# The first compression matmul with its operands exchanged: window tokens stationary in four column groups

## What is computed

```python
CMP_LEN, CMP_STRIDE, CMP_HIDDEN = 32, 16, 256        # S = 256 tokens, HEAD_DIM 64, G = 2 groups
n_cmp = (S - CMP_LEN) // CMP_STRIDE + 1              # 15 windows
cmp_idx = cmp_start[:, None] + np.arange(CMP_LEN)[None, :]

def compress(t, pe, w1, w2):
    blk = t[:, cmp_idx] + pe[:, None, :]
    blk = jnp.moveaxis(blk, 3, 2).reshape(B, n_cmp, G, CMP_LEN * D)
    return jax.nn.gelu(blk @ w1) @ w2

kc = rope_partial(compress(k_cmp, cmp_pos_k, cmp_wk1, cmp_wk2), pos[:, cmp_end])
vc = compress(v_cmp, cmp_pos_v, cmp_wv1, cmp_wv2)
```

## Time and profile before

| | us |
|---|---|
| median of 3 runs | 2285.81 |
| the three runs | 2283.96, 2285.81, 2295.26 |
| span of the profiled execution | 2275.8 |
| PE busy | 1985.1 (87%) |
| DVE busy | 871.2 (38%) |
| ACT busy | 735.0 (32%) |

### The profile page before, as it was taken

How to read it: one execution, slowest core, us unless ns; L and a number is a source line. 1 busy time by engine, 2 the same in 40 slices (tenths; PEclk the granted TensorE clock), 3 DMA queues, 4 the chain that set the end, 5 groups by cost and what they waited for, 6 DMA issues and landing times.

```text
span 2275.8 us, 29449 instructions
## 1 busy us (share of the span) xinstructions
PE 1985.1 (87%) x11980; PEld 1551.8 (68%) x11980; DVE 871.2 (38%) x1464; ACT 735.0 (32%) x1018; POOL 119.3 (5%) x112
## 2 busy tenths in 40 slices
PE   7967798888898777999988879987799998797997
PEld 5844443334443377778887879877787888797986
DVE  3052121111221232533355756533343335575653
ACT  1230011111111132557345434322255634533432
POOL 0000000000000000320210000000031030000000
PEclk9987899999999975999999989998599999998999
DMA  5403588988988732223223334543123322342452
GB/s 208 178 1 157 233 352 337 379 368 360 375 361 359 321 139 107 75 98 126 78 109 148 130 114 180 202 168 141 75 75 111 112 111 101 123 148 112 186 192 102
DMA packets 30887, 412.36 MB, mean 181 GB/s; under 512 B 3600, under 2 KB 5040, under 8 KB 5808
## 3 DMA queue, kind: packets, MB, share of 16 engines
q1 hardware_dynamic: 30768, 410.68, 46.0%
HBM read 408.84 MB, written 1.84 MB: 180 GB/s over the span
## 4 chain that ended last, share of the span: by engine, by line
issue 86%; PE 6%; POOL 5%; DVE 1%; DMA 1%; ACT 0%; SPq 0%; POOLq 0%; DVEq 0%; ACTq 0%
POOL work_mem L1650 5%; PE bank L703 3%; PE bank L711 2%; DMA work_mem<-in_const 1%; PE bank L798 0%; PE bank L735 0%; PE bank L780 0%; POOL small L1658 0%; PE bank L737 0%; PE bank L738 0%; DVE ht_mem L1689 0%; PE bank L773 0%; DVE work_mem L1809 0%; POOL small L1631 0%; DVE work_mem L1826 0%
## 5 line engine op out<-in xcount | busy, mean ns | idle before, releaser
L926 PE MATMUL bank<-wring,gates_mem 128*64 128x512 f32 x1024 | 238.5, 623 | 47.3 <-DMA wring<-in_w 40.7
L2012 DVE TENSOR_TENSOR w_lo<-wring,w_hi 128x2048 fp32r<-128x2048 f32 x88 | 201.3, 2292 | 188.2 <-ACT w_hi L1445 188.2
L1445 ACT ACTIVATE w_hi<-wring 128x2048 fp32r<-128x2048 f32 x88 | 168.5, 1915 | 303.4 <-PE bank L1002 171.8
L1001 PE MATMUL bank<-mixed_hi,w_hi_early 128*128 128x256 f32 x960 | 243.7, 291 | 6.8 <-DVE mixed_lo L2020 4.2
L1445 ACT ACTIVATE w_hi_early<-wring 128x2048 fp32r<-128x2048 f32 x80 | 152.9, 1912 | 265.3 <-PE bank L1002 176.1
L1002 PE MATMUL bank<-mixed_lo,w_hi_early 128*128 128x256 f32 x960 | 238.3, 285 | 0.0
L2012 DVE TENSOR_TENSOR w_lo<-wring,w_hi_early 128x2048 fp32r<-128x2048 f32 x80 | 183.2, 2290 | 124.7 <-ACT w_hi_early L1445 124.7
L926 PEld LDWEIGHTS bank<-wring,gates_mem 128*64 128x64 f32 x1024 | 88.4, 143 | 192.3 <-issue 192.3
L1006 PE MATMUL bank<-mixed_hi,w_lo 128*128 128x256 f32 x1472 | 208.8, 285 | 0.0
L1001 PEld LDWEIGHTS bank<-mixed_hi,w_hi_early 128*128 128x128 f32 x960 | 186.3, 194 | 12.3 <-issue 6.1
L1006 PEld LDWEIGHTS bank<-mixed_hi,w_lo 128*128 128x128 f32 x1472 | 192.2, 194 | 0.0
(11 more groups left out here) (404 smaller groups left out, 3216.2 us busy)
## 6 DMA issues: line engine op xcount, KB each, us to landing
wring<-in_w SPq DMA_DIRECT2D x192, 2048.0 KB, 8.4
cst<-in_const SPq DMA_DIRECT2D x1, 1273.0 KB, 7.6
prm<-in_prm SPq DMA_DIRECT2D x3, 381.0 KB, 8.5
x_mem<-in_x SPq DMA_DIRECT2D x1, 1024.0 KB, 4.9
out_x<-x_mem SPq DMA_DIRECT2D x1, 1024.0 KB, 3.9
rel_skew<-work_mem SPq DMA_DIRECT2D x1, 768.0 KB, 3.5
work_mem<-in_prm SPq DMA_DIRECT2D x1, 512.0 KB, 12.3
work_mem<-rel_skew SPq DMA_DIRECT2D x1, 512.0 KB, 3.6
```

What stands on the lines that cost most here:

```text
L926: mm = pe.matmul(out[half, :], x_e[:, pair, k, half], w[e][:, k, :], start=(k == 0), stop=(k == KT - 1))
L1001: pe.matmul(out, w[0][:, k, cols], x[0][:, k, :], start=(k == 0), stop=False)
L1445: act.activation(hi, w, ACT.Copy).then_inc(hi_ready, 1)
L2012: dve.tensor_tensor(lo, w, hi, ALU.subtract).then_inc(lo_ready, 1)
```

## The change

In each `hid` job the operands are exchanged. The stationary operand is now the windows' tokens: 31 columns, the 15 windows of either group and one meaningless window between them; the moving operand is a row block of the weights, 256 columns. The 16 steps of the contraction go in turn to four column groups q of the array, whose results lie in PSUM partitions 32q to 32q+30 of the same bank; each group adds up four steps. The four partial sums have to be added and turned, since they are windows x hidden and the rest of the kernel wants hidden x windows. ACT copies each of them, 31x256, into its 32 partitions of a new tile `hid_parts` (in `gates_mem`), and two new jobs `hsum` multiply a 128-column half of it, stationary, by a constant 0/1 matrix `winsum` (128x30) as the moving operand, which has a one where partition mod 32 is the window's row. The result is the 128x60 bank that was there before, and ACT copies it as before. DVE sets `hid_parts` to zero at the start of each layer, since partition 31 of each group is never written. The table of constants grows by the 30 columns of `winsum` and is loaded by the same DMA.

```diff
     ("negtriu", 256), ("gla", 7 * 128), ("rope", 128), ("dup", 256), ("inv", 1), ("cmpmask", 2 * N_CMP),
-    ("rowvalid", 2), ("iota", CAP), ("neghalf", 8), ("ones8", 8), ("one", 1), ("bucket", 384))
+    ("rowvalid", 2), ("iota", CAP), ("neghalf", 8), ("ones8", 8), ("one", 1), ("winsum", 2 * N_CMP), ("bucket", 384))
...
+    c[:, CONST["winsum"]] = row % 32 == (np.arange(2 * N_CMP) + np.arange(2 * N_CMP) // N_CMP)[None]
...
-                        ("rope_k", 1), ("dup", 2), ("hid", 2), ("kc", 1), ("vc", 1), ("rope_c", 1), ("gla_la", 1),
+                        ("rope_k", 1), ("dup", 2), ("hid", 2), ("hsum", 2), ("kc", 1), ("vc", 1), ("rope_c", 1), ("gla_la", 1),
...
-    pc_T = view(gates_mem, 6144, HEADS, S)
+    pc_T, hid_parts = view(gates_mem, 6144, HEADS, S), view(gates_mem, 0, 2, CMP_HIDDEN)
...
                 pe.wait_ge(dup_ready, 8 * l + 4 * n + 4)
                 free(j, l)
+                for step in range(4):
+                    for q in range(4):
+                        k = 4 * step + q
+                        win = dup[:, 2 * n + k // 8, :].rearrange("p (c s) -> p c s", s=CMP_STRIDE)
+                        mm = pe.matmul(psum[j.bank][32 * q:32 * q + 2 * N_CMP + 1, 0:CMP_HIDDEN],
+                                       win[:, k // 8:k // 8 + 2 * N_CMP + 1, 2 * (k % 8)], w[:, k, :],
+                                       start=(step == 0), stop=(step == 3))
+                mm.then_inc(bank_full[j.bank], 1)
+            for n, j in enumerate(layer["hsum"]):
+                parts_read = layer["hid"][n]
+                pe.wait_ge(bank_read[parts_read.bank], parts_read.count(l))
+                free(j, l)
                 for half in range(2):
-                    for k in range(16):
-                        win = dup[:, 2 * n + k // 8, :].rearrange("p (g c s) -> p g c s", g=2, s=CMP_STRIDE)
-                        mm = pe.matmul(psum[j.bank][:, half * 30:half * 30 + 30].rearrange("p (g c) -> p g c", g=2),
-                                       w[:, k, half * P:(half + 1) * P],
-                                       win[:, :, k // 8:k // 8 + N_CMP, 2 * (k % 8)], start=(k == 0), stop=(k == 15))
+                    mm = pe.matmul(psum[j.bank][:, half * 2 * N_CMP:(half + 1) * 2 * N_CMP],
+                                   hid_parts[:, n, half * P:(half + 1) * P], C("winsum"), start=True, stop=True)
                 mm.then_inc(bank_full[j.bank], 1)
...
+            act.wait_ge(hid_parts_clear, l + 1)
             for n, j in enumerate(layer["hid"]):
+                full(j, l)
+                for q in range(4):
+                    rows = slice(32 * q, 32 * q + 2 * N_CMP + 1)
+                    ins = act.activation(hid_parts[rows, n, :], psum[j.bank][rows, 0:CMP_HIDDEN], ACT.Copy)
+                ins.then_inc(bank_read[j.bank], 1)
+            for n, j in enumerate(layer["hsum"]):
                 full(j, l)
                 act.activation(hid_c[:, n].rearrange("p a b -> p (a b)"), psum[j.bank][:, 0:4 * N_CMP], ACT.Copy).then_inc(bank_read[j.bank], 1)
...
             norm_x(2 * l + 4, xn_a)
+            dve.memset(flat2(hid_parts), 0.0).then_inc(hid_parts_clear, 1)
             split_lo(0)
...
-            for j in last_in_bank(layer["hid"]):
+            for j in last_in_bank(layer["hsum"]):
                 dve.wait_ge(bank_read[j.bank], j.count(l))
```

More of the change, by code:

```diff
@@ L531, in program @@
     y_hi_ready, y_lo_ready, h2_hi_ready = sem("branch_high_ready"), sem("branch_low_ready"), sem("h2_high_ready")
+    hid_parts_clear = sem("window_sums_clear")
     layer = plan_layer(moe)
@@ L1705, in _ @@
         heads8 = lambda v: v.rearrange("p i (h e) -> p (i h) e", e=P)
+        flat2 = lambda v: v.rearrange("p a b -> p (a b)")
         dve.wait_ge(x_loaded, 16)
```

## The result

| | before, us | changed, us | ratio, 95% interval |
|---|---|---|---|
| first comparison (4 and 4 runs) | 2290.53 | 2251.51 | 0.9833 (0.9803 to 0.9862) |
| with e8 (13 and 2 runs) | 2286.82 | 2242.57 | 0.9808 (0.9764 to 0.9852) |
| with e13 (17 and 6 runs) | 2283.95 | 2251.90 | 0.9848 (0.9819 to 0.9878) |

The change makes the kernel 32 to 44 us faster by the medians, 39 in the first comparison; the 44 rest on two runs. The forecast was 31.4 us less, 2254.4, and the range 2246 to 2271; the measured 2251.5 lies in it. But the stage did not do what the prediction's main case said of it.

A forecast was written before the change was run, and what follows sets the result against it. PE alone was taken to bound the first compression matmul's stretch, 25.65 us in layer 1. 2 x (16.2 - 0.46) - 0.1 = 31.4 us off 2285.8 gave 2254.4 us; range 2246 to 2271.

The forecast's parts named there:

- the prediction's main case: First compression matmul: two passes under way at a time at clock 1.00; 2254.4 us in all, chance 0.60.
- The stage bounds the chain: First compression matmul: from first pass to ACT's second copy PE works alone, 25.65 us in layer 1.
- the sign: Prediction wrong if the distance from first compression pass to first attention score shrinks by less than the passes do.
- Passes, 7.3 us a layer: First compression matmul: 64 passes, two at a time, 33 x 0.22 = 7.3 us (bounds 7.1 and 7.8).
- rival (1): First compression matmul: all four column groups at once, passes 3.8 us a layer, kernel 2247.4 us; chance 0.12.
- Clock 1.00 in the stage: New compression passes run at full granted clock; falling and coming back would cost about 1.7 us more.
- Copies, +1.2: ACT's four 31x256 copies of the second bank are exposed: 1.2 us a layer (1.1 to 1.5).
- 0/1 matmul, +0.9: After the last copy: four passes of 30 columns, first latency and two wakes, 0.9 us (0.7 to 1.3).
- Memset, 0.46 on the path: DVE's clearing at the start of a layer is not hidden: 0.46 us in each layer (0 to 0.5).
- The stretch to the second 60-column copy: From first compression pass: 7.3 + 1.2 + 0.9 = 9.4 us instead of 25.65, gain 16.2 in each layer.
- After it, nil: Small steps up to the first attention scores: possible 0.5 us gain and up to 1.7 lost, put at nil.
- Nothing given back behind: Behind the stage no gain is lost to chunk waits or attention's clock; the rival, 2276 to 2286 us, had 0.06.

The follow-up runs named there:

- e8: The changed kernel, unchanged, run again for a second profile: 2242.6 us (2 runs).
- e13: The changed kernel, unchanged, run again in more rounds: 2251.9 us, 0.9848 of the kernel before.
- e1: The changed kernel with its two loops exchanged, so each column group's four steps stand in a row: 2257.9 us (2 runs).
- e6: The changed kernel with two steps of a column group in a row: 2246.9 us (2 runs).
- e11: The changed kernel with three steps of a column group in a row: 2246.5 us (1 run).
- e3: The changed kernel with one column group instead of four and one copy of 31x256 for a bank: 2262.2 us (2 runs).
- e7: The kernel before, unchanged, run again for a second profile: 2279.6 us (1 run).

## Why the prediction was right, and where not

- *The stage bounds the chain*: right. PE's passes became 20.2 and 21.6 us shorter, and after the new copies and the 0/1 matmul the first score came 18.6 and 20.0 us sooner. The prediction called itself wrong if this distance shrank by less than the passes do. By the letter that happened, but its own sum had 16 against 18 too, since the copies and the 0/1 matmul stand between; the sign was ill put.
- *Passes, 7.3 us a layer*: the term that failed, by almost two. The step was "matmuls start in order. Four groups in that order still give two at a time". Measured 3.9 to 4.0 at full clock, rival (1)'s 3.8: four at a time. The rows of L940 could not tell, as the prediction said; I had settled it by an argument about order, and e1, e6 and e11 show that a pass does go ahead of waiting passes of another group.
- The Trainium skill ("TensorE: Matmul & The Clock Gate", Part 3: Packing small matmuls) says that distinct column groups start some 4 ns apart; here the first four passes of a stage started 6 to 7 ns apart. The same part of the Trainium skill says that matmuls start strictly in program order; by e1's and e11's starts they do not across column groups. It says in one place that a load overlaps a running matmul only in other row groups, and in another that it may also go to a background weight buffer; in e3 all loads take the same rows, and a pass started every 0.216 us, against 0.215 for 256 columns by L940's rows, so the first of the two does not hold here.
- *Clock 1.00 in the stage*: right in five of the six layers profiled; in layer 1 of the first profile it was 0.50 for 3.4 us, which the prediction had named as a sign of being wrong, and cost 1.4 us. The 1.7 us allowed for such a case stood on no row of the kernel before.
- *Copies, +1.2*: 1.53. The 0.27 us from one start to the next held for an ACT copy followed by other work; four alike start 0.385 apart.
- *0/1 matmul, +0.9*: 0.80 (886.10 less 883.77, where the passes end, less 1.53). *Memset, 0.46 on the path*: it lasts 0.48 us, but PE starts only 0.24 and 0.33 later.
- The stretch to the second 60-column copy was put at 9.4 us and was 7.70 and 6.35, so the gain of the stretch 18.0 and 19.3 instead of 16.2. *After it, nil*: the small steps gained 0.64 us a layer. In layer 1 it is their first few, which now run at 1.00; in layer 2 half is there and half just ahead of the first score, where the clock is up again.
- *Nothing given back behind*: most likely wrong, by 2 to 3 us a layer, see e7 and e8. The total came out near the sum partly by luck, because two errors stood against each other: 3 us a layer too little for the groups, and 2 to 3 us a layer for the clock in the attention part. It also helped that the forecast was taken from a median of 2285.8; the gain in the first comparison was 39.0 us against the 31.4 of the sum.
- The chances for a result inside 11.4 us of no change add up to 0.08, not 0.07, and for slower to 0.02; nothing hangs on it.

## What to carry to other kernels

A matmul with few moving columns pays for its weight load (0.11 us for 30 columns here, at full clock), and its price doubles where the clock falls, as it did here under 30 and 60 columns: let the wide operand move, and judge it at the clock that it will get. With at most 32 stationary columns, four column groups took little over a quarter of the time (3.9 us against 14.03), provided that no group gets more than four passes in a row (two f32 matmuls). Partial sums are copied for the price of one copy if the copy spans all partitions and the 0/1 matrix masks the rest, as long as the rest is finite.

## What the runs showed of the hardware that I had not expected

- Passes to different column groups do not keep program order: a fifth pass in a row for one group holds up everything behind it (8.37 us for runs of eight passes, 5.79 for six, 3.97 for four, 3.9 to 4.0 for two).
- An f32 moving operand with a stride of 64 bytes, repeated four times, streamed 120 columns in 0.208 us, 1.7 ns a column, where 256 contiguous ones took 0.216, 0.84 ns a column. At half the clock a pass of them took 0.213 us, hardly more. Whether the stride or the repeat does it was not tried apart.
- 64 passes at 1.00 (14.03 us) and 128 at half the clock (25.6 us) did the same work; the same kernel's attention part took 421.8 or 427.5 us by where the clock fell.
